# A decoder layer on one core: the first head's level operands ahead of a slab's rest, and one wait a tile for both halves of its weights

## What is computed

```
a = rmsnorm(h)
z = a @ w_in              # q, f, i, gates of 8 HGRN2 heads; q, k, v, gates of 4 GLA heads; two merge gates
log_f, log_a = gates of f and of a rank-16 product
o_h, s_h = gated_recurrence(silu(zq), k_h, zi, log_f, s0)     # 8 heads
o_g, s_g = gated_recurrence(q_g, k_g, v_g, log_a, s0)         # 4 heads
y_h = (rmsnorm(o_h) * silu(zg)) @ w_hgrn_up ;  y_g likewise @ w_gla_up
h = h + rmsnorm((sigmoid(m_h) * y_h + sigmoid(m_g) * y_g) @ w_out)
u = square(relu(rmsnorm(h) @ w_ff1)) ;  h = h + rmsnorm(u @ w_ff2)
h = h + sigmoid(h @ w_ple_gate) * (p @ w_ple)
```

## Time and profile before

| | us |
|---|---|
| median of three runs | 1627.98 |
| lowest and highest | 1627.93, 1628.76 |
| the profiled execution itself | 1629.61 |
| its span | 1627.8 |
| TensorE busy in it | 1620.3 |
| DVE, ScalarE busy | 1110.0, 842.0 |

### The profile page before, as it was taken

One profiled execution on the slowest core, in us unless ns is written; L12 is line 12 of the kernel. 1 busy time (PEld: TensorE's weight loads), 2 busy tenths in 40 slices (PEclk: granted clock), 3 DMA queues, 4 the chain that ended last, 5 costly groups with the idle time before them and its releaser, 6 DMA issues.

```text
span 1627.8 us, 35049 instructions
## 1 busy us (share of the span) xinstructions
PE 1620.3 (100%) x13332; PEld 1615.9 (99%) x13332; DVE 1110.0 (68%) x1917; ACT 842.0 (52%) x1192; POOL 185.9 (11%) x166
## 2 busy tenths in 40 slices
PE   9999999999999999999999999999999999999999
PEld 9999999999999999999999999999999999999999
DVE  7548767888888876655986665566555665555774
ACT  7575765666665665434664334443444334443452
POOL 4101001111111100055300000000000000035200
PEclk9999999999999999999999999999999999999999
DMA  9478895565555567855675865588557775555564
GB/s 276 164 230 223 269 265 174 162 192 162 191 167 182 153 203 229 273 180 184 173 216 187 248 208 180 187 260 241 177 180 242 242 223 186 180 194 179 172 192 144
DMA packets 151178, 329.17 MB, mean 202 GB/s; under 512 B 16944, under 2 KB 79536, under 8 KB 150608
## 3 DMA queue, kind: packets, MB, share of 16 engines
q1 hardware_dynamic: 143888, 326.00, 64.7%
q10 hardware_dynamic: 7232, 2.43, 0.6%
HBM read 310.08 MB, written 18.30 MB: 202 GB/s over the span
## 4 chain that ended last, share of the span: by engine, by line
PE 96%; DMA 1%; DVE 1%; ACT 0%; issue 0%; SPq 0%; ACTq 0%; DVEq 0%
PE bank L380 28%; PE bank L381 28%; PE bank L382 28%; PE bank L398 3%; PE bank L400 3%; PE bank L403 3%; DMA raw<-in_stream 1%; PE bank L768 1%; DVE wlo L360 0%; PE bank L795 0%; PE bank L787 0%; PE bank L766 0%; ACT whi L355 0%; PE bank L788 0%; PE bank L757 0%
## 5 line engine op out<-in xcount | busy, mean ns | idle before, releaser
L355 ACT CAST whi<-raw 128x1024 fp32r<-128x1024 f32 x532 | 547.8, 1049 | 472.0 <-PE bank L382 396.1
L380 PE MATMUL bank<-a_hi,whi 128*128 128x264 f32 x2576 | 734.3, 285 | 0.1
L381 PE MATMUL bank<-a_lo,whi 128*128 128x264 f32 x2576 | 729.8, 283 | 0.0
L382 PE MATMUL bank<-a_hi,wlo 128*128 128x264 f32 x2576 | 729.4, 283 | 0.0
L360 DVE TENSOR_TENSOR wlo<-raw,whi 128x1024 fp32r<-128x1024 f32 x518 | 629.8, 1247 | 112.5 <-ACT whi L355 111.4
L380 PEld LDWEIGHTS bank<-a_hi,whi 128*128 128x128 f32 x2576 | 485.2, 188 | 0.8 <-issue 0.7
L381 PEld LDWEIGHTS bank<-a_lo,whi 128*128 128x128 f32 x2576 | 485.5, 188 | 0.1
L382 PEld LDWEIGHTS bank<-a_hi,wlo 128*128 128x128 f32 x2576 | 482.9, 187 | 0.0
L380 PE MATMUL bank<-b_hi,whi 128*128 128x264 f32 x1280 | 363.1, 284 | 0.0
L381 PE MATMUL bank<-b_lo,whi 128*128 128x264 f32 x1280 | 362.6, 283 | 0.0
L382 PE MATMUL bank<-b_hi,wlo 128*128 128x264 f32 x1280 | 362.4, 283 | 0.0
(11 more groups left out here) (222 smaller groups left out, 1507.3 us busy)
## 6 DMA issues: line engine op xcount, KB each, us to landing
raw<-in_stream SPq DMA_DIRECT2D x532, 512.0 KB, 4.7
m_spill<-stage SPq DMA_DIRECT2D x32, 132.0 KB, 3.7
lev<-m_spill SPq DMA_DIRECT2D x16, 264.0 KB, 2.8
room<-in_x SPq DMA_DIRECT2D x7, 528.0 KB, 7.3
S<-in_state_hgrn SPq DMA_DIRECT2D x6, 512.0 KB, 6.5
out_new_hgrn_sample<-S SPq DMA_DIRECT2D x6, 512.0 KB, 6.7
S<-in_state_gla SPq DMA_DIRECT2D x5, 512.0 KB, 6.6
out_new_gla_sample<-S SPq DMA_DIRECT2D x5, 512.0 KB, 6.8
```

Of the source, the lines that this page charges most:

```text
L355: act.copy(whi[:, s, :], raw[:, s, :]).then_inc(hi_ready, 1)
L380: pe.matmul(out, whi[:, s, w], hi[:, k0 + k, :], start=start and k == 0, stop=False)
L381: pe.matmul(out, whi[:, s, w], lo[:, k0 + k, :], start=False, stop=False)
L382: mm = pe.matmul(out, wlo[:, s, w], hi[:, k0 + k, :], start=False, stop=stop and k == HT - 1)
```

## The change

Two edits. First, in DVE's order for the first head alone, all 16 products of the level operands and the kd product go ahead of slab(2); for the other heads the order stays. Second, `tile` waits once, after the wait for the bank, until both halves of the tile have their rests, and `multiply`, called from there with `ready=True`, waits no more. The heads and the up stage call `multiply` without it and wait at each half as before.

```diff
--- before.py
+++ after.py
@@ -367,10 +367,11 @@
         at = slice(P, end)
         dve.tensor_tensor(wlo[:, s, at], raw[:, s, at], whi[:, s, at].bitcast(F32), ALU.subtract).then_inc(done, 1)
 
-    def multiply(pe, T, par, half, out, hi, lo, k0, start, stop, before_k=None, midway=None, at=HT // 2):
+    def multiply(pe, T, par, half, out, hi, lo, k0, start, stop, before_k=None, midway=None, at=HT // 2, ready=None):
 
         s = slot_of(par, half)
-        pe.wait_ge(lo_ready, 2 * T + (half + 1))
+        if not ready:
+            pe.wait_ge(lo_ready, 2 * T + (half + 1))
         for k in range(HT):
             if before_k:
                 before_k(k0 + k)
@@ -385,10 +386,11 @@
     def tile(pe, T, par, hi, lo, first=False, before_half=None, before_k=None, bank=None):
         if not first:
             pe.wait_ge(tiles_drained, T - 1)
+        pe.wait_ge(lo_ready, 2 * T + 2)
         for half in range(2):
             if before_half:
                 before_half(half)
-            multiply(pe, T, par, half, (bank or MM)[par][:, 0:TOK], hi, lo, half * HT, half == 0, half == 1, before_k)
+            multiply(pe, T, par, half, (bank or MM)[par][:, 0:TOK], hi, lo, half * HT, half == 0, half == 1, before_k, ready=True)
 
     def wide(pe, T, hi, lo, ready, base, n, free=None, norm=None):
 
@@ -1543,19 +1545,31 @@
                 dve.tensor_tensor(lq, lq, rights(q_b[:], h), ALU.mult)
                 return dve.tensor_tensor(cells(k_lev[:, l - 1, :], h, 0, h, 2 * h), lk, lefts(k_b[:], h), ALU.mult)
 
+            def first_levels():
+
+                dve.wait_ge(h_sem["kq_ready"], now(H))
+                dve.wait_ge(h_sem["lev_exp"], now(H))
+                for l in range(LEVELS // 2):
+                    level_operands(l)
+
+            def last_levels():
+
+                for l in range(LEVELS // 2, LEVELS):
+                    last = level_operands(l)
+                last.then_inc(h_sem["lev_ready"], 1)
+                dve.wait_ge(h_sem["kd_exp"], now(H))
+                dve.tensor_tensor(kd[:], kd[:], k_b[:, 0:NP_TOK], ALU.mult).then_inc(h_sem["kd_ready"], 1)
+
+            if opening:
+                first_levels()
+                last_levels()
             slab(2)
-
             gate_tile(0)
-            dve.wait_ge(h_sem["kq_ready"], now(H))
-            dve.wait_ge(h_sem["lev_exp"], now(H))
-            for l in range(LEVELS // 2):
-                level_operands(l)
+            if not opening:
+                first_levels()
             slab(3)
-            for l in range(LEVELS // 2, LEVELS):
-                last = level_operands(l)
-            last.then_inc(h_sem["lev_ready"], 1)
-            dve.wait_ge(h_sem["kd_exp"], now(H))
-            dve.tensor_tensor(kd[:], kd[:], k_b[:, 0:NP_TOK], ALU.mult).then_inc(h_sem["kd_ready"], 1)
+            if not opening:
+                last_levels()
             slab(4)
             slab(5)
             if D == 1:
```

## The result

| | before | after |
|---|---|---|
| median (lowest to highest) of ten runs | 1628.21 (1627.93 to 1630.30) | 1632.55 (1632.28 to 1636.44) |
| the profiled execution | 1629.61 | 1632.39 |
| its span | 1627.8 | 1630.6 |

The ratio is 1.0026, 95% interval 1.0018 to 1.0034: the changed kernel is slower, by 4.3 us between the medians. The forecast was 2.7 us slower, 1630.7 us, with a range up to 1632.4; the median lies 0.15 us above it. Between the two profiled executions, however, the difference is 1632.39 - 1629.61 = 2.78 us, close to the 2.73 of the forecast's sum. So there are two things to explain: the 2.8, and why the medians stand 4.3 apart.

What follows compares the result with a forecast made beforehand. TensorE, running for the whole span, was taken to bound the kernel. Stops of 3.96 us less a 1.23 us gain gave +2.73 us; set against the median 1627.98, the forecast was 1630.7 us, range 1628.8 to 1632.4.

Steps and rivals of the forecast that it cites:

- the term of edit 1: First head: moving the level operands and kd product ahead removes TensorE's wait before the level products, gaining 1.23 us.
- the nine stops: One wait a tile makes TensorE stop in tiles 10, 12, 14, 16, 22, 26, 28, 131, 133: 3.96 us lost.
- The wait of the first head: TensorE's 1.0 us stop before the level products, released by DVE's last level operand; removing it gains 1.23 us.
- Chain of even tiles: Tiles 12, 14, 16: late starts make the next even tile's rests late, 0.39 us each, 1.17 together.
- the rival that it is used up once: Tiles 12, 14, 16 cost nothing behind tile 10's stop: -1.17, giving +1.6, 1629.6 us; within a 0.12 chance.
- Tile 22: Second half's rests, behind the big subtraction, end after the tile's start: a stop costing 0.63 us.
- Tiles 10, 26 and 131: Stops of TensorE on the second half's rests at these tiles' starts, costing 0.71, 0.62 and 0.13 us.
- Restart is dearer: Rival: each of 9 stops costs 0.28, not 0.16, and more tiles stop: +4.0, 1632.0 us; chance 0.25.
- Removed waits: Middle waits of 177 tiles, worth nothing; rival says 0.04 us each, result -4.3 us, 1623.6; chance of faster 0.03.
- The chances: Odds given for the whole change: faster 0.03, same 0.72, slower 0.25, with 0.2%, 3.3 us, as the limit.

Runs made afterwards that it cites:

- edit 2 alone: The kernel before with only the one wait a tile, the first head keeping its old order; median 1632.69 us, ratio 1.0023.

## Why the prediction went wrong, point by point

**What failed: the term of edit 1 set against the median.** The prediction put -1.23 us for edit 1 and then said: "the median of the three runs shown is 1.63 lower, 1627.98. Set against it the forecast is 1630.7 us". The term was read from one execution. Against that execution it holds: the sum gave 1632.34 us, and the changed kernel's profile took 1632.39. That the two agree within 0.05 us is partly luck: the stops were 0.24 dearer and small steps lost 0.15, while the opening stretch and the start of tile 43 gave 0.2 and 0.14 that nobody had forecast. The profiled execution was 1.63 us above the median of three, and 1.24 of that was the very wait that edit 1 was to remove; taking it from the median counted it twice. (The stop of 0.14 at tile 43 is in none of the other five profiles of before.) With the 0.24 us that the wait costs on average in the last four profiles of before in place of 1.23, the sum is 3.96 - 0.24 = +3.7 and the forecast 1631.7 (over all six profiles the average is 0.52, and it would be 1631.4); with the nine stops as measured, 4.20 - 0.24 = 4.0, 1631.9. The median of ten runs of before was 0.23 above that of three; the last 0.4 us to 1632.55 stay open, where the medians of before alone ranged from 1628.21 to 1629.17 between sets of runs.

**The wait of the first head** was said to hang on the order of the operands, and the stops behind it on TensorE's earlier work. The moved operands fitted as forecast: 3.2 us for 16, kd done when the rest of tile 43 could start, TensorE not later. That the wait hung on how long two loads took as well, and was worth only 0 to 0.94 us in the other five profiles, was missed. ScalarE's 4.03 us in DVE's row was read as cover for the operands and not followed back to the load that made it long.

**The stops.** All nine are where they were forecast, and no tenth. Chain of even tiles: right, 0.39 to 0.41 each for 0.39, and shown by the run with one wait in these tiles only; the rival that it is used up once fell. Tile 22: exact. Tiles 10, 26 and 131 cost 0.08, 0.07 and 0.07 more, 0.24 in all with the rest. A restart cost 0.16 at tile 12 (80.53 - 0.12 - 80.25), as taken from the earlier trace rows, but 0.22 at tile 10 (68.52 - 0.12 - 68.18).

**Restart is dearer**, the rival with 0.28 a stop, holds only in part; the nine were 0.03 dearer on average and not 0.12. Read in this way from the three profiles with one wait in every tile (the changed kernel twice, edit 2 alone), a restart cost 0.16 us at tiles 12, 14, 16, 22, 28 and 133, which the kernel runs in loops (`tiles`), and 0.22 at tiles 10, 26 and 131, which it writes out one by one. The rival had expected the dearer ones in the loops. With the waits of each half put back it is 0.23 in the loops and 0.18 at tiles 10 and 26. The cause of this pattern was not tested. The result came out on the rival's side, above 0.2%, by another mechanism.

**Removed waits** were put at nothing, and this is shown from both sides: 354 added ones cost nothing away from the stops, 128 removed ones gave nothing. The Trainium skill, page "TensorE: Matmul & The Clock Gate", section "Step-by-step: what each phase is for", gives about 62 ns for each matmul that the sequencer handles in its own code. If a wait cost as much, 354 more would be 22 us, an estimate from this page; the run shows 0.3.

**The chances.** 0.25 for slower by over 0.2% was too little: the median ratio is 1.0026, though its interval begins at 1.0018. The range ended 0.15 us too low, because it let the stops vary and not the wait that edit 1 removes.

## What to carry to other kernels

A wait found in one profile is only worth its length if the other executions have it: look at how the profiled time stands to the median first, and where it is above, ask whether the wait is that excess. Then follow the releaser back; if a load ends the chain, look in other executions how long that load takes there. Delaying the engine that waits need not help: here the loads wait, through rests and roundings, for slabs that it has multiplied, and came later by as much as it did. One wait for two buffers costs nothing where the second is early and saves nothing either, but where it is late and the producers hang on the consumer, the loss comes back every round.

## What the runs showed of the hardware

- A wait of TensorE that is already met costs no time: three in a tile and one in a tile differ by 0.3 us over 177 tiles, all of it where TensorE stopped anyway, and 128 waits fewer gave nothing.
- A stop on a rest costs TensorE 0.16 us beyond the end of the releasing instruction in tiles run in a loop and 0.22 in tiles written out: 0.05 to 0.15 to the next matmul's start, and a second step of 0.19 to 0.23 in place of 0.12. With the waits of each half behind it, 0.07 more in loops and 0.04 less at tiles 10 and 26.
- A TensorE that runs late makes its loads late too in this ring: tile 40's first half was issued 3.89 us later where TensorE was 3.89 us late.
- The same 512 KB load at the same place of the same kernel landed after 7.85 to 10.62 us over six executions.
